# 1088 columns of peer_v dense and 960 gathered, the slabs' low parts on GpSimd

## What is computed

```python
u = jnp.take(peer_u, i_blk, axis=0)
a = jax.nn.gelu(jnp.einsum("td,thkd->thk", x_blk, u)) * g_blk
v = jnp.take(peer_v, i_blk, axis=0)
return jnp.einsum("thk,thkd->td", a, v)
```

## Time and profile before

| | us |
|---|---|
| median of 3 runs | 3046.98 (3043.51 to 3047.13) |
| the profiled execution | 3037.15 |
| its span | 3035.3 |
| the 128 slabs, from 2558.8 to 3019.2 | 460.4 |

### The profile page before, as it was taken

One profiled execution on the slowest core, in us unless ns is written; L12 is line 12 of the kernel. 1 busy time (PEld: TensorE's weight loads), 2 busy tenths in 40 slices (PEclk: granted clock), 3 DMA queues, 4 the chain that ended last, 5 costly groups with the idle time before them and its releaser, 6 DMA issues.

```text
span 3035.3 us, 36596 instructions
## 1 busy us (share of the span) xinstructions
PE 2624.6 (86%) x13061; PEld 2225.5 (73%) x13061; DVE 2162.4 (71%) x3281; ACT 1419.6 (47%) x2694; POOL 833.2 (27%) x563
## 2 busy tenths in 40 slices
PE   7999999999999999999999998887434007999997
PEld 6777878888888878888778898777433006888886
DVE  4996465454554565565455568999999988998887
ACT  5466454343433454545554443222199925333333
POOL 0000000010100000000000003766688875765563
PEclk9999999999999999999999999999755558999999
DMA  9544555555555546546435567999999997999997
GB/s 256 181 153 140 181 190 183 193 182 196 191 188 191 189 165 217 183 161 203 161 120 172 190 226 259 419 419 419 415 416 420 420 419 261 408 408 408 407 407 298
DMA packets 278140, 805.40 MB, mean 265 GB/s; under 512 B 33113, under 2 KB 73281, under 8 KB 243936
## 3 DMA queue, kind: packets, MB, share of 16 engines
q1 hardware_dynamic: 220400, 417.26, 40.7%
q0 software_dynamic: 57344, 385.91, 31.3%
q10 hardware_dynamic: 240, 0.18, 0.0%
HBM read 799.09 MB, written 4.19 MB: 265 GB/s over the span
## 4 chain that ended last, share of the span: by engine, by line
PE 36%; DMA 8%; POOL 7%; issue 5%; DVE 4%; ACT 1%; DVEq 0%; POOLq 0%
POOL expert_rows L2123 7%; PE ps L2667 7%; PE ps L222 6%; PE ps L223 6%; PE ps L224 6%; DMA expert_rows<-in_peer_u,index 5%; PE ps L2675 1%; PE ps L2674 1%; PE ps L2676 1%; DMA expert_slabs<-in_peer_v 1%; DVE junk L2560 1%; PE ps L2209 1%; PE ps L2207 1%; PE ps L2208 1%; DMA expert_pieces<-in_peer_v,const 1%
## 5 line engine op out<-in xcount | busy, mean ns | idle before, releaser
L207 DVE TENSOR_TENSOR wl<-ring,wh 128x1024 fp32r<-128x1024 f32 (+2 forms) x616 | 732.8, 1232 | 629.0 <-ACT wh L195 626.6
L195 ACT CAST wh<-ring 128x1024 fp32r<-128x1024 f32 (+2 forms) x612 | 605.6, 1040 | 628.1 <-PE ps L224 571.6
L2123 POOL DMA_INDIRECT expert_rows<-in_peer_u,index x256 | 477.1, 1864 | 588.8 <-DVE wl L207 429.6
L222 PE MATMUL ps<-wh,th 128*128 128x512 f32 (+1 forms) x1464 | 576.4, 394 | 6.3 <-DVE wl L207 4.4
L224 PE MATMUL ps<-wh,tl 128*128 128x512 f32 (+1 forms) x1464 | 568.5, 388 | 0.0
L223 PE MATMUL ps<-wl,th 128*128 128x512 f32 (+1 forms) x1464 | 568.3, 388 | 0.0
L2560 DVE CUSTOM_DVE_ANT_0 junk<-expert_rows,h 128x2048 f32<-128x2048 f32 x217 | 493.9, 2292 | 37.8 <-DMA expert_rows<-in_peer_u,index 36.4
L222 PEld LDWEIGHTS ps<-wh,th 128*128 128x128 f32 x1464 | 275.7, 188 | 66.4 <-DVE wl L207 6.4
L224 PEld LDWEIGHTS ps<-wh,tl 128*128 128x128 f32 x1464 | 275.5, 188 | 56.6
L223 PEld LDWEIGHTS ps<-wl,th 128*128 128x128 f32 x1464 | 275.7, 188 | 54.1
L2599 DVE SCALAR_TENSOR_TENSOR x_and_pieces<-expert_pieces,const,x_and_pieces 128x896 f32<-128x896 f32 x256 | 289.7, 1148 | 32.8 <-DMA expert_pieces<-in_peer_v,piece_index 17.2
(11 more groups left out here) (408 smaller groups left out, 4442.6 us busy)
## 6 DMA issues: line engine op xcount, KB each, us to landing
ring<-in_w_in SPq DMA_DIRECT2D x80, 1024.0 KB, 5.1
expert_slabs<-in_peer_v SPq DMA_DIRECT2D x128, 576.0 KB, 9.2
ring<-in_w_up SPq DMA_DIRECT2D x64, 1024.0 KB, 5.1
ring<-in_w_down SPq DMA_DIRECT2D x64, 1024.0 KB, 5.0
ring<-in_w_in SPq DMA_DIRECT2D x68, 512.0 KB, 4.7
ring<-in_w_out SPq DMA_DIRECT2D x32, 1024.0 KB, 5.0
ring<-in_w_peer_q SPq DMA_DIRECT2D x16, 1024.0 KB, 5.1
ring<-in_w_ukv SPq DMA_DIRECT2D x8, 1024.0 KB, 5.5
```

The source lines that it names most:

```text
L195: self.nc.scalar.copy(self.wh[:, i % 2, two, 0:w], self.ring[:, i, two, 0:w]).then_inc(self.high_ready, 1)
L207: self.nc.vector.tensor_tensor(self.wl[:, i % 2, two, 0:w], self.ring[:, i, two, 0:w], self.wh[:, i % 2, two, 0:w].bitcast(F32), ALU.subtr ...
L222: mm(o, hi, wh, start=start and k == 0, stop=False)
L2123: nc.gpsimd.indirect_dma_start(p.rows[:, n % GR, :], None, peer_u, bass.IndirectOffsetOnAxis(ap=p.index[:, n:n + 1], axis=0)).then_inc(p.l ...
```

## The change

`PIECE` becomes 960 and `WHOLE` 576, so a slab has 1088 columns (544 KB), its float32 parts are 288 columns each, and a gathered piece has 960 (480 KB). `SPLIT` stays 512. The subtraction that makes the slab's low part leaves DVE and goes to POOL, with a semaphore of its own, `slab_low`. POOL's requests are no longer asked for as soon as a buffer is free: for each slab m POOL waits for the slab's high part, subtracts, and then asks for the pieces up to 24 + 240 m / 128.

```diff
-    PIECE, WHOLE, SPLIT = 896, 640, 512
+    PIECE, WHOLE, SPLIT = 960, 576, 512
...
-        summed = place("x_and_pieces", [P, NH, PIECE], at=-85 * KB)
+        summed = place("x_and_pieces", [P, NH, PIECE], at=-86 * KB)
...
-            for n in range(UNITS * TOPK):
+
+            def ask(n):
                 if n >= GR:
                     pool.wait_ge(piece_used, n - GR + 1)
                 nc.gpsimd.indirect_dma_start(
                     pieces[:, n % GR, :], None, v_pieces,
                     bass.IndirectOffsetOnAxis(ap=piece_at[n % NH][:, n // NH:n // NH + 1], axis=0)
                 ).then_inc(piece_landed[n % GR], 16)
+
+            asked = 0
+            for m in range(-1, NKEYS):
+                if m >= 0:
+                    pool.wait_ge(split_high, 3 * m + 3)
+                    nc.gpsimd.tensor_tensor(v_split[:, m % 2, 1, :], slabs[:, m % SLOTS, WHOLE:],
+                                            v_split[:, m % 2, 0, :].bitcast(F32), ALU.subtract).then_inc(slab_low, 1)
+                upto = GR + P // 8 + (NH * PICKS - P // 8) * m // NKEYS if m >= 0 else GR + P // 8
+                upto = min(upto, NH * PICKS) if m < NKEYS - 1 else NH * PICKS
+                for n in range(asked, upto):
+                    ask(n)
+                asked = upto
...
-                dve.wait_ge(split_high, 3 * m + 3)
-                nc.vector.tensor_tensor(v_split[:, m % 2, 1, :], slabs[:, m % SLOTS, WHOLE:],
-                                        v_split[:, m % 2, 0, :].bitcast(F32), ALU.subtract).then_inc(split_low, 1)
...
-                pe.wait_ge(split_low, 3 * m + 3)
+                pe.wait_ge(split_low, NH * (m + 1))
+                pe.wait_ge(slab_low, m + 1)
```

More of the change, by code:

```diff
@@ L2417, in peer_stage @@
             "row_quarters_turned", "row_quarters_laid", "rows_dotted")
-        distances_made, split_high, split_low = core.new("distances_made", "experts_high", "experts_low")
+        distances_made, split_high, split_low, slab_low = core.new("distances_made", "experts_high", "weights_low", "slab_low")
         cols_hot = core.new("cols_hot_low", "cols_hot_high")
```

## The result

The changed kernel is slower: 3083.78 us (median, 3075.02 to 3089.85) against 3046.99, a ratio of 1.0124, 95% interval 1.0113 to 1.0136. That is +37 us. The forecast was 3164, +117: the right sign, three times the size. The measured time lies inside the range that I gave for 8 in 10, 3062 to 3228, but only because that range reached down into the first rival. The profiled execution took 3075.02, the fastest of the four, its span 3073.2 against 3035.3.

A forecast was written before the change was run, and what follows sets the result against it. PE (3.53 us a slab) bounds the kernel, DMA right behind; POOL and DVE colliding give 128 x 4.5 + 4 = 580 against 460.4, +120, +1, -4: +117, so 3154 profiled, 3164 median; 8-in-10 range 3062 to 3228.

The forecast's parts named there:

- first rival: 128-slab stage: gathers don't collide with DVE's additions; 3.7 to 4.1 us a slab, +50, 3097 us; chance 0.2.
- DMA's 0.07 us a slab: Slab stage: 1.479 MB a slab at 408 GB/s takes 3.62 us, 0.07 more than now; +9 if DMA bounds.
- additions: DVE in the slab stage: 64 more columns add 0.07 us to each addition's 1.07, giving 1.14.
- subtraction: POOL in the slab stage: making the slab's low part costs 1.0 us, like the MLP's square; bounds 1.0 to 2.0.
- sum of exclusive time: Slab stage: DVE's 2.63 and POOL's subtraction of 1.0 fill 3.63 us a slab, before waits for each other.
- late requests: Slab stage: pieces asked for behind the next slab's subtraction might land late; taken at 0, 0.5 us kept for range.
- how the waits close into a loop: Slab stage: POOL and DVE collide, 4.75 us with two additions, 3.7 with one; mean 4.62, lower figure 4.2, taken 4.5.
- mean gather of 1.18: Slab stage before the change: gathers average 1.18 us against 0.94 free, cited as evidence against gathers not colliding.
- forecast's pace: Slab stage: 4.5 us a slab taken; the loop of collisions restated as 4.3 and more, +90, for the move alone.

The follow-up runs named there:

- e1: Kernel before with only the columns changed (960 gathered, 1088 dense), low part still on DVE, requests unpaced: 3045.28 us, ratio 1.0025.
- e2: Changed kernel with the columns back at 896 gathered and 1152 dense, subtraction and paced requests on POOL: 3122.68 us, ratio 1.0283.
- e5: Changed kernel with 928 gathered and 1120 dense columns: 3128.49 us, ratio 1.0289.
- e8: e2 plus a one-column memset on DVE in each slab, between low parts and first addition: 3121.18 us, ratio 1.0277.
- e3: Kernel before with POOL's requests paced by the slab's high part, but no subtraction on POOL: 3037.95 us, ratio 1.0003.
- e7: Changed kernel without the addition of x to the dense columns at slab 96 and without its load: 3063.65 us, ratio 1.0115.
- e9: e2 plus a 128-column memset on DVE in each slab, between low parts and first addition: 3094.22 us, ratio 1.0191.
- e6: Changed kernel with 1024 gathered and 1024 dense columns: 3113.41 us, ratio 1.0242.

## Why the forecast was wrong

**What bounded the kernel** was right: PE, with DMA right behind it. e1 measured +8.2 where DMA's 0.07 us a slab gave +9.

**The parts.** The additions, 1.14 us forecast, came at 1.145. The subtraction holds DVE for 1.09 and takes 1.27 by itself, where I took 1.0 for both. The sum of exclusive time, 3.63 forecast, is 0.20 + 0.27 + 1.09 + 1.875 x 1.145 = 3.71, and the pace is 3.79. That a gather waits for an addition with two SBUF inputs was right as well: in e2, e5 and e8 about half of all requests take over 1.3 us. I read the earlier trace rows as if it showed this of tensor_tensor, but the DVE operation there is another one. Only these runs show it of tensor_tensor, by the first request of a slab: it takes 1.07 and ends 0.79 behind the second low part. The late requests, taken at nothing, cost nothing in the fast pattern (DVE waited for a piece for 1.2 us in 400), and e3 confirms the pacing.

**The step that failed** is "how the waits close into a loop". I started that timetable with an addition left over behind the subtraction and the first request behind that addition, and DVE's low parts tied to ACT's casts. No run goes by that timetable: e2, whose pace it hit, gets there by long requests on POOL, and only 4 of its 93 subtractions from 2600 to 3000 took over 1.4. In the changed kernel's fast pattern DVE lags so far that casts are always ready, the first request meets only the short low part (1.07 us, not 2.2), and the second slips in between two additions (0.94). POOL then reaches its next subtraction before DVE's low parts, and the two hardly leave a gap: a slab takes 3.79 where I forecast 4.5. I listed this as the first rival, 3.7 to 4.1 us a slab and 3097 us, with a chance of 0.2; it was the case for about 100 slabs, and a slab of some 4.5 for part of the rest. POOL's sum shows where the time went: without x (e7) 1.36 + 1.875 x 1.06 + 0.44 = 3.79, against 4.31 in e2; a request of 1.06 in place of 1.36 makes the difference. What I gave as the evidence against it, the mean gather of 1.18, was taken from a stage in which requests came at any time; here they come at one fixed distance from DVE's operations, and a mean over random distances says nothing of that.

I also priced the two edits as if they added. They don't: the wider addition is what lets the second request in. The move costs 86 us beside additions of 896 columns, and about 29 beside those of 960 (37 less 8). That my forecast's pace came out in e2 (4.3 us a slab, +90 expected, +85.6 measured) is in part luck, since its timetable didn't; and what divides e2 from the change is 0.06 us, a request 0.03 behind the end of an addition or 0.03 ahead of it.

## What to carry to other kernels

Two engines that take turns on a shared resource can have more than one periodic timetable, and here a few hundredths of a microsecond in one operation chose between them. Where a sum of exclusive times comes to nearly the whole period, forecast the sum and the slow timetable as two cases, and find what event each request is tied to instead of taking a mean wait. An operation moved to an engine that shares the resource isn't moved off it: 0.60 us of DVE's time became 1.09. And a pause is worth what it moves, not what it lasts.

## What the runs showed of the hardware

A gather on POOL, 0.94 us when free, took 1.84 to 1.92 when it was issued up to 0.04 us behind the recorded end of an addition on DVE that reads two SBUF tensors, with the next addition queued already, and 0.95 when it was issued 0.01 to 0.04 ahead of that end. The edge lies within 0.01 us of the recorded end. It looks as if the one that asked first gets the next turn, but that is not the whole rule: four of the requests in the table took 2.35 to 2.40 and ended 0.75 behind the second low part, behind three operations of DVE; and in the slab of e2 above, the second low part began 0.55 ahead of the subtraction (2705.80 and 2706.35) and ended behind it.

"SBUF — State Buffer" of the Trainium skill, § Who interferes with whom, calls the shared pair an exclusive lock; the 1.36 us low part behind the subtraction agrees. It also says that tensor_tensor was not seen to stall software DMAs. Here requests of such DMAs wait for SCALAR_TENSOR_TENSOR on DVE for up to a whole addition, and for the low parts, which are TENSOR_TENSOR, and the measurement decides.

A memset between the low parts and the first addition moved the end of that addition by far less than it lasts: 0.014 us for one column (0.06 us long) and for 64 (0.11), 0.027 for 128 (0.165).

What stays open is where exactly the edge lies, since requests at the same distance from the recorded end won in e9 and e6 and lost in e5, and how often other executions of the changed kernel fall into the slow pattern. Their spread of 15 us (3075 to 3090) would fit it, but only the fastest was profiled.
